# Rotary turn: the pair swap moved from a VectorE shuffle to a TensorE matmul with a constant matrix

## The reference, cut to what matters

```python
def axial_rope(n_tok, rot_dim, dtype):
    ...
    ang = jnp.concatenate([r[:, None] * inv, cc[:, None] * inv], axis=-1)
    return jnp.cos(ang).astype(dtype), jnp.sin(ang).astype(dtype)

def apply_rope(x, cos, sin):
    x1, x2 = x[..., 0::2], x[..., 1::2]
    cos, sin = cos[:, None, :], sin[:, None, :]
    return jnp.stack([x1 * cos - x2 * sin, x1 * sin + x2 * cos], axis=-1).reshape(x.shape)

# layers 0 and 3
    q_l = apply_rope(q_l.reshape(bsz, n_lat, A_HEADS, A_HEAD_DIM), cos, sin)
    k_l = apply_rope(k_l.reshape(bsz, n_lat, A_KV_HEADS, A_HEAD_DIM), cos, sin)
# layer 1
    q_l = jnp.concatenate([q_l[..., :B_NOPE], apply_rope(q_l[..., B_NOPE:], cos, sin)], axis=-1)
    kpe_l = apply_rope(kpe_l[:, :, None, :], cos, sin)[:, :, 0]
```

## Time and profile before

| | before |
|---|---|
| median of 3 runs | 2369.76 us |
| the profiled execution's own time | 2369.76 us |
| span of its records | 2368.0 us |
| PE busy (matmuls) | 2230.5 us, 94% of the span |
| DVE busy | 1214.8 us, 51% |
| ACT busy | 642.7 us, 27% |
| mean granted TensorE clock | 0.985 of full speed |

### The profile page before, as it was taken

One profiled execution on the slowest core, in us unless ns is written; L12 is line 12 of the kernel. 1 busy time (PEld: TensorE's weight loads), 2 busy tenths in 40 slices (PEclk: granted clock), 3 DMA queues, 4 the chain that ended last, 5 costly groups with the idle time before them and its releaser, 6 DMA issues. The chain is left out here.

```text
span 2368.0 us, 29454 instructions
## 1 busy us (share of the span) xinstructions
PE 2230.5 (94%) x10368; PEld 1194.9 (50%) x10369; DVE 1214.8 (51%) x2847; ACT 642.7 (27%) x1469; POOL 36.5 (2%) x45
## 2 busy tenths in 40 slices
PE   7998899999999989999999899999999999999997
PEld 3445686478744558777867643333333323333332
DVE  2989558453895683636742453443334333333333
ACT  3108542443211363346332321111111111111111
POOL 0000000000000000000001000000000000000000
PEclk9999999999999999999999899999999999999999
DMA  9662034301477002231240389989989998998997
GB/s 382 248 236 82 1 143 174 119 1 38 177 269 283 16 1 107 107 107 37 72 169 9 146 320 422 421 338 422 421 358 422 421 421 358 422 421 358 422 421 329
DMA packets 115126, 569.66 MB, mean 241 GB/s; under 512 B 11840, under 2 KB 13888, under 8 KB 57312
## 3 DMA queue, kind: packets, MB, share of 16 engines
q1 hardware_dynamic: 115040, 568.53, 60.1%
HBM read 567.45 MB, written 1.05 MB: 240 GB/s over the span
## 5 line engine op out<-in xcount | busy, mean ns | idle before, releaser
L2886 PE MATMUL PS<-BIG,PW 128*64 128x512 f32 x2304 | 513.8, 595 | 27.1 <-DMA BIG<-in_w 26.3
L2886 PEld LDWEIGHTS PS<-BIG,PW 128*64 128x64 f32 x2304 | 159.5, 137 | 371.9 <-issue 290.8
L3127 DVE TENSOR_SCALAR PW<-PS 128x512 f32<-128x512 f32 x36 | 24.9, 692 | 486.0 <-PE PS L2886 486.0
L2925 PE MATMUL PS<-BIG,PW 128*64 128x512 f32 x1152 | 255.4, 595 | 8.6 <-ACT PW L2762 8.6
L2759 ACT ACTIVATE PW<-PW 128x512 f32<-128x512 f32 x36 | 22.7, 630 | 736.1 <-DVE PW L3127 736.1
L400 DVE SCALAR_TENSOR_TENSOR BIG<-BIG,COND_ROWS 128x1024 f32<-128x1024 f32 x128 | 153.4, 1221 | 25.7 <-DMA BIG<-in_w_ada_columns 25.4
L2925 PEld LDWEIGHTS PS<-BIG,PW 128*64 128x64 f32 x1152 | 79.2, 137 | 161.1 <-issue 143.9
L1145 PE MATMUL PS<-HT,BIG 128*128 128x512 f32 (+1 forms) x448 | 152.0, 501 | 0.0
L1145 PEld LDWEIGHTS PS<-HT,BIG 128*128 128x128 f32 x448 | 85.1, 190 | 65.3 <-issue 60.3
L692 PE MATMUL PS<-HT,BIG 128*128 128x256 f32 x512 | 111.6, 379 | 1.4 <-PEq L894 1.4
L1540 PE MATMUL PS<-BIG,HT 128*128 128x512 f32 x256 | 110.0, 592 | 0.0
(11 more groups left out here) (533 smaller groups left out, 3112.3 us busy)
## 6 DMA issues: line engine op xcount, KB each, us to landing
BIG<-in_w SPq DMA_DIRECT2D x384, 1024.0 KB, 17.5
BIG<-in_l_w_in SPq DMA_DIRECT2D x20, 2048.0 KB, 8.6
BIG<-in_l_w_ada_columns SPq DMA_DIRECT2D x40, 1024.0 KB, 7.2
BIG<-in_w_ada_columns SPq DMA_DIRECT2D x24, 1024.0 KB, 7.3
BIG<-in_l_w_out SPq DMA_DIRECT2D x8, 2048.0 KB, 8.2
BIG<-in_w_in SPq DMA_DIRECT2D x7, 2048.0 KB, 8.2
BIG<-in_l_w_ada SPq DMA_DIRECT2D x4, 2048.0 KB, 15.3
BIG<-in_w_out SPq DMA_DIRECT2D x2, 2048.0 KB, 7.8
```

Of the source, the lines that this page charges most:

```text
L2886: ins = nc.tensor.matmul(PS[64 * g:64 * g + 64, 4 + half, :], xt[:, c % 4, c // 4, :], W[:, c, half * F + g * 512:half * F + g * 512 + 512 ...
L2925: ins = nc.tensor.matmul(PS[64 * g:64 * g + 64, 7, :], at_[:, k % 4, k // 4, :], W[:, 8 + k // 2, k % 2 * D + g * 512:k % 2 * D + g * 512 ...
```

## The change

The shuffle is taken out of `rope_turn`. A constant 128x128 matrix `swap` (one signed entry in each row, plus one row up or down) is added to the table of constants, and the sign leaves the `sin` table. PE multiplies each tile by it: `rope_mix`, one float32 matmul of 256 columns into bank 4 or 5 in turn. DVE then waits for `rope_mixed`, multiplies that bank by `sin` into `tmp` and raises `rope_taken`, multiplies the tile by `cos` in place, and adds.

In each of the three blocks PE gets a function `rope(n)` that waits until ACT has taken the n-th turned tile, and from the third on until DVE has read the bank two turns back (`rope_taken`, n - 1). In layer 0 `rope(0)`, `rope(1)` and `rope(2)` stand ahead of tile 4, and `rope(n)` after tile n + 1; in layer 3 `rope(n)` stands after tile n + 4; in layer 1 `rope(0)` after the square sums, with a wait for tile 5's eviction, and the other four after tiles 13 to 16.

```diff
 tabs["eps"] = np.full((P, 1), EPS)
+swap = np.zeros((P, P))
+swap[p[1::2], p[0::2]] = -1.0
+swap[p[0::2], p[1::2]] = 1.0
+tabs["swap"] = swap
...
-    tabs["sin"] = np.sin(ang).T[(p % 64) // 2] * np.where(p % 2, 1.0, -1.0)[:, None]
+    tabs["sin"] = np.sin(ang).T[(p % 64) // 2]
...
-        def rope_turn(dve, x, tmp):
-
-            x = x[:, 0:LAT]
-            dve_chain.add(nc.vector.stream_shuffle(tmp, x, [r ^ 1 for r in range(32)]))
-            shuffled = dve_chain.n
-            dve_chain.add(nc.vector.tensor_tensor(x, x, const("cos"), ALU.mult))
-            dve.wait_ge(dve_chain.sem, shuffled)
-            dve_chain.link(dve, nc.vector.tensor_tensor(tmp, tmp, const("sin"), ALU.mult))
-            dve_chain.link(dve, nc.vector.tensor_tensor(x, x, tmp, ALU.add))
+        def rope_mix(x, n):
+
+            nc.tensor.matmul(PS[:, 4 + n % 2, 0:LAT], const("swap"), x[:, 0:LAT], start=True, stop=True).then_inc(
+                S["rope_mixed"].sem, 1)
+
+        def rope_turn(dve, x, n, tmp):
+
+            dve.wait_ge(*at("rope_mixed", n + 1))
+            nc.vector.tensor_tensor(tmp, PS[:, 4 + n % 2, 0:LAT], const("sin"), ALU.mult).then_inc(S["rope_taken"].sem, 1)
+            dve_chain.link(dve, nc.vector.tensor_tensor(x[:, 0:LAT], x[:, 0:LAT], const("cos"), ALU.mult))
+            dve.wait_ge(*at("rope_taken", n + 1))
+            dve_chain.link(dve, nc.vector.tensor_tensor(x[:, 0:LAT], x[:, 0:LAT], tmp, ALU.add))
...
+                    def rope(n):
+                        kind, m, _, _, _ = tiles[roped[n]]
+                        pe.wait_ge(*at("tile_taken", roped[n] + 1))
+                        if n >= 2:
+                            pe.wait_ge(*at("rope_taken", n - 1))
+                        rope_mix((qt if kind == "q" else kt_)[:, m, :], n)
...
                             ins.then_inc(done[j][0], 1)
+                        if later + 1 <= j <= later + len(roped):
+                            rope(j - 1 - later)
...
                         if kind == "z" and m == 2:
                             square_sums()
+                            pe.wait_ge(*at("tile_taken", 6))
+                            rope(0)
+                        if j - 1 in roped[1:]:
+                            rope(roped.index(j - 1))
```

More of the change, by code:

```diff
@@ L271, in layers_and_experts_kernel @@
         names = ("vectors_loaded first_loaded early_loaded0 early_loaded1 early_summed cond_rows_ready tokens_loaded consts_loaded late_loaded transposed transposed_taken cond_ready squares_ready squares_added "
[L272 removed]
+                 "square_sum_ready rms_ready inverse_ready rstd_ready scaled_ready tile_ready tile_taken rope_mixed rope_taken "
                  "scores_ready max_ready exp_ready scores_used probs_ready probs_turned turned_copied heads_ready "
@@ L1192, in _ @@
                         dve.wait_ge(*at("tile_taken", j + 1))
-                        rope_turn(dve, (qt if kind == "q" else kt_)[:, m, :], tmp)
+                        rope_turn(dve, (qt if kind == "q" else kt_)[:, m, :], n, tmp)
                         if not pending:
@@ L1216, in window_layer @@
             S["tile_taken"].passed(len(tiles))
+            S["rope_mixed"].passed(len(roped))
+            S["rope_taken"].passed(len(roped))
             ws.done = first + 5
@@ L1284, in _, with rope @@
                 def _(pe):
+                    def rope(n):
+                        kind, m, _ = tiles[roped[n]]
+                        pe.wait_ge(*at("tile_taken", roped[n] + 1))
+                        if n >= 2:
+                            pe.wait_ge(*at("rope_taken", n - 1))
+                        rope_mix(kpe if kind == "kpe" else qr[:, m, :], n)
                     def square_sums():
@@ L1380, in _ @@
                         dve.wait_ge(*at("tile_taken", j + 1))
-                        rope_turn(dve, kpe if kind == "kpe" else qr[:, m, :], tmp)
+                        rope_turn(dve, kpe if kind == "kpe" else qr[:, m, :], n, tmp)
                         if n == 0:
@@ L1391, in latent_layer @@
             for n, k in (("a_ready", 3), ("b_ready", 2), ("inverse_ready", 2), ("rstd_ready", 2),
-                         ("scaled_ready", 3)):
+                         ("scaled_ready", 3), ("rope_mixed", len(roped)), ("rope_taken", len(roped))):
                 S[n].passed(k)
```

1 line of the change is left out of this document (removed).

## The result

| | before | after |
|---|---|---|
| median | 2369.28 us (4 runs, 2368.50 to 2372.54) | 2395.78 us (4 runs, 2387.64 to 2398.79) |
| ratio of the runs | | 1.0104, 95% interval 1.0078 to 1.0131 |
| profiled execution, its span | 2369.76, 2368.0 us | 2398.98, 2397.2 us |
| mean granted clock, profiled execution | 0.985 | 0.978 |

The changed kernel is 26.5 us slower by the medians, 1.0% by the ratio, where 16.9 us (0.7%) were forecast, and 2395.78 lies above the range. Its runs differ by 11 us among themselves, and their mean granted clock goes against their time: 2387.64 us at 0.984, 2395.21 to 2398.79 at 0.977 to 0.979. The first question is whether the terms of the sum are right.

A forecast was written before the change was run, and what follows sets the result against it. PE, almost fully busy in all three streams, was taken as the bound, or 0.40 us from it. 2369.76 + 10.8 (matmuls) + 4.0 (wait) - 0.4 (covered by DVE) + 2.5 (clock) = 2386.7 us; range 2382.3 to 2390.5.

The forecast's parts named there:

- PE's streams set the end in all three blocks: Layers 0, 1 and 3: PE's matmul stream sets the block's end, or is 0.40 us from it.
- the 0.4 us that DVE covered: End of layer 0's block: DVE ended it before, so the first 0.40 us of PE's delay is not seen.
- 25 matmuls at 0.432, 10.8 us: Layers 0, 1 and 3: each new float32 matmul costs PE 0.432 us, 10.8 us together, all on the path.
- rival 4: The new matmuls pass in a quarter of their form's time, 2.7 us in place of 10.8: 2378.6 us; chance 0.02.
- The wait, 4.0 us: Layer 0, at tile 4: PE idles 4.0 us until DVE reads the bank of turn 0; bounds 3.5 and 4.3.
- Rival 2: DVE holds PE at every turn of layer 0; 4.2 us more if DVE took 8.0, 2390.9 us; chance 0.05.
- The clock behind the wait, 2.5 us: Layer 0, tile 4 and after: half clock behind PE's new idle stretch loses 2.5 us; bounds 0 and 3.4.
- Rival 1: Layer 0: the clock holds through PE's 4.0 us idle stretch, 2.5 us less, 2384.2 us; chance 0.15.
- Rival 3: DVE sets the end and the matmuls are covered; blocks shorten by up to 8.3 us, 2361.5 us; chance 0.04.
- The blocks longer by 2.2 and 4.3 us: Layers 1 and 3: the blocks grow by 2.2 and 4.3 us and no more; growth beyond their matmuls would refute it.
- nothing is absorbed, nothing grows: Later stages: expert loads start behind finished matmuls, so a later PE makes them later by as much.
- About 0.2%, 4.7 us: Whole kernel: the difference that a measurement can tell from no change; chance of a result within it 0.03.

The follow-up runs named there:

- e1: Changed kernel with layer 0's new matmuls from the third on two tiles later and DVE's column sums dealt out anew, so PE needn't wait; 2383.77 us, ratio 1.0044.
- e3: Kernel before, turns untouched, plus 25 float32 128x256 matmuls that nobody reads at the changed kernel's places on PE; 2383.47 us, ratio 1.0043.
- e13: Kernel before plus 28 independent 128x256 matmuls in one place of layer 0's stream, ahead of tile 12, no wait; 2382.12 us, ratio 1.0046.
- e2: Changed kernel with eight more 128x256 float32 matmuls ahead of the third new matmul's wait in layer 0; 2391.87 us, ratio 1.0075.
- e7: Kernel before with one added wait of PE ahead of layer 0's tile 4 for DVE's first turn, no matmul added; 2379.17 us, ratio 1.0024.
- e11: Changed kernel with layer 0's turns left on DVE with the shuffle, 15 matmuls in layers 1 and 3 alone; 2378.98 us, ratio 1.0033.
- e8: Kernel before plus 16 independent 128x256 matmuls in one place of layer 0, ahead of tile 12, no wait; 2377.95 us, ratio 1.0018.
- e4: The changed kernel, unaltered, measured a second time; 2393.27 us, ratio to before 1.0084.
- e10: The changed kernel, unaltered, measured a third time beside the kernel before on the same chip; 2390.79 us, ratio 1.0082.
- e12: Kernel before with about half the earlier filler matmuls that nobody reads, ahead of PE's waits where it idles; 2371.61 us, ratio 0.9997.
- e9: The kernel before, unaltered, measured again with a second profile; 2371.62 us, ratio 1.0006.
- e16: Second profile of the kernel before with 16 independent matmuls in one place of layer 0; one execution, 2378.23 us.

## Why the prediction was wrong

By its own steps, with what the runs showed:

- *PE's streams set the end in all three blocks.* Right. In e1, e3 and e13 the block of layer 0 grew by the added matmuls less the 0.4 us that DVE covered: with each trace's earlier start taken out, the attention's shift is 3.9, 3.9 and 11.7 us for 10, 10 and 28 matmuls at 0.432.
- *25 matmuls at 0.432, 10.8 us.* Right in layers 0 and 3; in layer 1 the five cost 2.9 and not 2.2 us, so 11.5 in all. The quarter price of rival 4 is excluded by e3. The Trainium skill, "TensorE: Matmul & The Clock Gate", section "Back-to-back issue gap", would have made them 2.7 us (an estimate by its formula); no run here agrees with it for float32.
- *The wait, 4.0 us.* Right: 3.9, once, released by DVE's first read of PSUM. Rival 2 is excluded: DVE waits 1.38 us for PE at the middle turns.
- *The clock behind the wait, 2.5 us.* Right in kind (e2 takes it away, e7 makes it by itself), 3.0 us in the first profile; 1.7 to 3.3 over the profiles. Rival 1 is excluded.
- *Rival 3*, DVE sets the end: excluded, all variants with added matmuls are slower.
- *The blocks longer by 2.2 and 4.3 us "and no more", and of the later stages "nothing is absorbed, nothing grows".* This is the step that failed. The sum counted the granted clock in one place and took every other stretch of the kernel before as fixed. They aren't fixed: in the first profile 12 us came from stages that the change doesn't touch, and the unchanged kernel alone lies between 2366.45 and 2378.74 us, its mean clock between 0.979 and 0.987.
- *"About 0.2%, 4.7 us, is what a measurement of this kernel can tell from no change."* Too little for a few runs: the changed kernel's three medians lie 19.8, 20.4 and 26.5 us above their before.

The fixed terms, that is what the blocks of layers 0, 1 and 3 themselves grow by, are then 10.8 + 2.9 + 4.3 = 18.0 us, where the sum had 16.9. What the medians say, each against the runs of before measured beside it:

| kernel | fixed terms | median over before |
|---|---|---|
| e11 layers 1 and 3 only | 7.2 | 8.6 |
| e1 no wait | 11.1 | 10.3 |
| e3 matmuls unread | 11.1 | 10.0 |
| e13 28 matmuls | 11.7 | 12.1 |
| e8 16 matmuls | 6.5 | 5.1 |
| e7 wait alone | 5.7 to 7.3 | 6.3 |
| e2 wait filled | 15.0 | 18.4 |
| e4, e10 changed kernel | 18.0 | 19.8, 20.4 |
| the first measurement | 18.0 | 26.5 |

The first six kernels come out within 1.5 us of their fixed terms. The two that have both the 25 matmuls and the later start of tile 4 do not: e2 lies 3.4 us above, the changed kernel 2 us in two measurements and 8.5 in the first one. The parts measured alone also add up to less than the whole: matmuls (e3) and wait (e7) are 10.0 + 6.3 = 16.3 us. With a standard error of 1 to 1.6 us in each of these differences, by the spread of the runs, this can still be chance.

Beside e1 to e12 there are 68 executions of before, 2366.45 to 2378.74 us with a median of 2372.2, and 15 of the changed kernel, 2387.64 to 2398.98 with a median of 2393.3. (Its 15 are e4, e10 and the first measurement, the profiled executions with them.) In both, time goes with the mean granted clock, 1.5 us for each 0.001 (a straight line through both sets with one slope). At 0.983 before takes 2374.1 us (median of 14) and after 2389.23 and 2390.28; at 0.984, 2370.6 (median of 21) and 2387.64. On the line the two kernels are 15.9 us apart at equal clock (standard error 0.6), close to the 15.0 of the matmuls and the wait alone. (The executions come from several chips; before's medians on them go from 2370.4 to 2373.5.) The mean clocks differ by 0.0036, 0.9836 against 0.9800; at 1.5 us for 0.001 that is 5.5 us more. About 3.0 of them are the stretch behind the new wait; the rest is the clock elsewhere.

So the first measurement had four runs of before of which none was above 2372.54, and four of after of which three were near 2397, at a clock of 0.977 to 0.979. Its 26.5 us can be taken apart with the medians of all executions: 18.0 are the fixed terms, 2.9 that its before was faster than 2372.2, 2.5 that its after was slower than 2393.3, and 3.1 what the changed kernel's 2393.3 has over 2372.2 + 18.0. The middle two, 5.4 us, are luck of the draw. Without them the difference would be about 21 us, and the top of the range is 20.7 above before (2390.5 - 2369.76); e4 and e10, at 19.8 and 20.4, lie just inside it. The forecast of 2386.7 was 3 to 4 us short of what the fixed terms give on the median of all runs of before (2372.2 + 18.0 = 2390.2), and the range ended at 2390.5, since it held no term for the spread of the clock. The spread could be asked for before: the trace of before has the clock at 0.50 in ten stretches, 74 us together, and three runs were no sample of them.

The Trainium skill says of this, in "TensorE: Matmul & The Clock Gate", section "Part 1: The HAM clock gate (the "warmup" mystery)", that the number of slow matmuls at the start of a kernel differs from run to run of the same kernel. The runs agree: the first stretch at 0.50 lasts 10.2, 10.2 and 6.8 us in the three profiles of before. They extend it to the middle of a program (e9 against the first profile, e16 against e8). The section "A second HAM failure mode: psum-queue depth-cycling" puts oscillation, in a bf16 kernel, down to small idle gaps between groups of matmuls; the two places that vary most here have such gaps: 1.05 us ahead of each of the last two transposes of layer 0's attention, 1.31 and 0.86 us at the end of the hybrid attention. No run here tried to close them.

What stays open: all three profiles of the changed kernel have the low clock in the output projection, for 6.8 us each, and e2 has it for 10.2, where the other kernels without fillers have it in three of eleven, for 3.4 us twice and 6.8 once. With the six of six in the hybrid attention this makes it likely that the changed kernel gets the low clock more often there, which would be the 2 to 3 us above its fixed terms, but the profiled executions of the changed kernel are among its slowest (2395.97, 2398.26 and 2398.98 us for a median of 2393.3), so they can't tell how often. Why it should is open.

## What to carry to other kernels

Price a moved operation by the stream that it enters: one small float32 matmul costs its full spacing on an engine that is 100% busy, and saving DVE time there buys nothing. Put such a matmul late enough that the engine never waits for its partner: e1 does the same work as the changed kernel and is 9.5 us faster. Of these, 6.9 us are shown: a wait of 4 us on a full engine costs itself and then a stretch at half clock. Before forecasting a change of 0.5%, ask how far single runs of the unchanged kernel lie apart and whether the granted clock explains it; the range must hold that spread, and two single profiles must not be subtracted where their low-clock stretches differ.

## What the hardware showed that I had not expected

- The same kernel gets the low clock in different stretches: in before's hybrid attention 13.7 + 6.8 us, 30.7 us, and 13.7 + 10.2 us in three profiles. Single runs of it lie up to 0.5% apart (2366 to 2379 us), the slower ones at the lower mean clock.
- The low clock lasted 30 us without a break, with PE busy for 26.29 of 30.50 us (e9), through work that ran partly at full clock in another execution of the same kernel.
- Raising the mean clock isn't a gain in itself: e12 ran at 0.985 to 0.990 and was as fast as before (ratio 0.9997). In the place shown above the fillers kept the clock up where PE was waiting anyway, and it fell in the work behind.
- The new matmul took 0.63 us instead of 0.43 among tiles with 64 columns of weights.
